# State mixing by halves, another order of its squares and subtractions, and the rotary key copies of the latents behind their squares

## What is computed

```
# layer 1: RWKV-7
xx = h_prev - h                                   # h is the normalised input, h_prev the row before
xr, xw, xk, xv, xa, xg = h + xx * mu[0..5]
r, k, v = xr @ w_r, xk @ w_k, xv @ w_v             # three 1024 x 1024 products
w_log = -softplus(-(w0 + tanh(xw @ w1) @ w2)) - 0.5   # low rank 64
a = sigmoid(a0 + (xa @ a1) @ a2)                   # low rank 64
g = sigmoid(xg @ g1) @ g2                          # low rank 128
kk = normalised per head (k * k_k);  k = k * (1 + (a - 1) * k_a)
# then the recurrence over 5 chunks of 64 frames

# layer 2: latent attention
cq, ckv, kpe = split(h @ w_in)
q = rmsnorm(cq) @ w_uq;  lat = rmsnorm(ckv);  kpe = rope(kpe)
k_nope, v = lat_all @ w_ukv;  logits = q_nope k_nope + q_pe kpe
```

## Times and profile before

| | us |
|---|---|
| timed executions | 1843.74, 1843.94, 1838.21 |
| median | 1843.74 |
| profiled execution | 1838.96 |
| its span, first to last instruction | 1837.0 |
| mean granted clock of TensorE, share of full speed | 0.961 |

### The profile page before, as it was taken

How to read it: one execution, slowest core, us unless ns; L and a number is a source line. 1 busy time by engine, 2 the same in 40 slices (tenths; PEclk the granted TensorE clock), 3 DMA queues, 4 the chain that set the end, 5 groups by cost and what they waited for, 6 DMA issues and landing times.

```text
span 1837.0 us, 37502 instructions
## 1 busy us (share of the span) xinstructions
PE 1683.1 (92%) x14117; PEld 1593.9 (87%) x14117; DVE 1169.8 (64%) x2070; ACT 856.0 (47%) x1602; POOL 731.5 (40%) x836
## 2 busy tenths in 40 slices
PE   4987999997987998999999888999999988999995
PEld 2876999995777997999999777899999876999994
DVE  3586677736467455677765538677765586677732
ACT  2344556533652343365633344465643444566532
POOL 5660466501024211266621245166621760466501
PEclk9998999998998999999999989999999998999998
DMA  6411555454230002455545211355546411555451
GB/s 158 125 48 48 159 138 159 125 150 140 71 113 29 4 10 75 118 157 140 146 142 173 71 58 47 95 158 148 141 135 172 131 48 47 156 142 156 127 145 60
DMA packets 342622, 205.04 MB, mean 112 GB/s; under 512 B 20898, under 2 KB 339640, under 8 KB 342384
## 3 DMA queue, kind: packets, MB, share of 16 engines
q1 hardware_dynamic: 338704, 196.35, 37.2%
q0 software_dynamic: 3808, 7.17, 1.4%
HBM read 200.00 MB, written 3.39 MB: 111 GB/s over the span
## 4 chain that ended last, share of the span: by engine, by line
PE 78%; DVE 10%; ACT 5%; issue 4%; POOL 3%; DMA 0%; ACTq 0%; POOLq 0%; DVEq 0%
PE bank L871 22%; PE bank L872 22%; PE bank L873 22%; PE bank L1170 4%; PE bank L882 2%; DVE lo L1940 1%; ACT hi L1468 1%; ACT LS L1502 1%; DVE LS L1985 1%; DVE LS L1994 1%; POOL vrows L627 1%; POOL lo L655 1%; PE bank L1194 1%; PE bank L938 1%; DVE xn L2174 1%
## 5 line engine op out<-in xcount | busy, mean ns | idle before, releaser
L871 PE MATMUL bank<-XH,hi 128*128 128x320 f32 (+1 forms) x1992 | 631.2, 317 | 20.8 <-DVE lo L1940 8.9
L1940 DVE TENSOR_TENSOR lo<-raw,hi 128x2048 fp32r<-128x2048 f32 (+3 forms) x201 | 425.1, 2115 | 317.1 <-ACT hi L1468 317.0
L872 PE MATMUL bank<-XL,hi 128*128 128x320 f32 (+1 forms) x1992 | 622.9, 313 | 0.0
L873 PE MATMUL bank<-XH,lo 128*128 128x320 f32 (+1 forms) x1992 | 622.0, 312 | 0.0
L871 PEld LDWEIGHTS bank<-XH,hi 128*128 128x128 f32 (+1 forms) x1992 | 378.7, 190 | 34.4 <-DVE lo L1940 17.7
L1468 ACT ACTIVATE hi<-raw 128x2048 fp32r<-128x2048 f32 (+4 forms) x205 | 359.6, 1755 | 75.3 <-PE bank L873 67.0
L872 PEld LDWEIGHTS bank<-XL,hi 128*128 128x128 f32 (+1 forms) x1992 | 379.1, 190 | 1.3
L873 PEld LDWEIGHTS bank<-XH,lo 128*128 128x128 f32 (+1 forms) x1992 | 378.7, 190 | 0.0
L691 POOL TENSOR_TENSOR upad<-upad,rstd 128x128 f32<-128x128 f32 (+1 forms) x176 | 167.2, 970 | 200.4 <-ACT upad L1548 200.4
L871 PE MATMUL bank<-GH,hi 128*128 128x322 f32 x704 | 219.2, 311 | 0.0
L872 PE MATMUL bank<-GL,hi 128*128 128x322 f32 x704 | 218.8, 311 | 0.0
(11 more groups left out here) (392 smaller groups left out, 2448.4 us busy)
## 6 DMA issues: line engine op xcount, KB each, us to landing
raw<-in_f_w_up SPq DMA_DIRECT2D x176, 512.0 KB, 4.9
raw<-in_f_w_down SPq DMA_DIRECT2D x64, 704.0 KB, 4.7
raw<-in_a_w_in SPq DMA_DIRECT2D x12, 1024.0 KB, 5.4
raw<-in_b_w_rkv SPq DMA_DIRECT2D x12, 1024.0 KB, 5.2
raw<-in_a_w_out SPq DMA_DIRECT2D x8, 1024.0 KB, 5.3
raw<-in_b_w_out SPq DMA_DIRECT2D x4, 1024.0 KB, 5.4
raw<-in_c_w_out SPq DMA_DIRECT2D x4, 1024.0 KB, 5.2
raw<-in_a_w_in SPq DMA_DIRECT2D x12, 256.0 KB, 4.3
```

Of the source, the lines that this page charges most:

```text
L871: pe.matmul(out, a, xh(k), start=(start and k == 0), stop=False)
L872: pe.matmul(out, a, xl(k), start=False, stop=False)
L873: last = pe.matmul(out, b, xh(k), start=False, stop=(stop and k == kt - 1))
L1940: dve.tensor_tensor(lo[n % 2][:, 0:w_], raw[n % 2][:, 0:w_], hi[n % 2][:, 0:w_].bitcast(F32), ALU.subtract).then_inc(w_lo, 1)
```

## The change

In state mixing:
- the six loads of the low-rank weights move from GpSimd's queue to SyncE's, behind the load of slab s0+1 and ahead of that of slab s0+2, with the same wait for the layer's input;
- VectorE normalises, subtracts and mixes four tiles and then the other four, and writes the rows of the shift state behind them; TensorE makes the low-rank products in the same two halves, ahead of the transposition of the shift rows;
- ScalarE applies the sigmoid (`middle(2)`) right behind `middle(1)` instead of behind the seven casts; the copy of the shift rows goes behind the casts;
- `key_squares(2)` and `(3)` go ahead of the split of slab s0+4, `(6)` and `(7)` ahead of four casts and the split of s0+5;
- `key_gain(0)` and `tile(12)` go between the two exponentials; GpSimd therefore waits for the second exponential at m = 0;
- `key_fans` are issued behind products 12, 13 and 14 as 2, 3 and 3 instead of 2, 2, 2, 2 behind 12 to 15; VectorE makes five `key_heads` ahead of the split of slab s0+8 instead of four, and `keys_and_rows(1)` behind the split of slab s0+9 instead of ahead of it.

In the latents GpSimd adds up the squares of `cq` before it copies the rotated keys, instead of after.

```diff
@@ SyncE @@
+            def low_rank_weights():
+                sp.wait_ge(x_done, 8 * xs_of[norm_of[1, "mix"]] + 8)
+                for dst, src in ((L1[:, :, 0:64], ...b_w1), (L1[:, :, 64:128], ...b_a1), (L1[:, :, 128:256], ...b_g1),
+                                 (L2[0:64, 0, :], ...b_w2), (L2[64:128, 0, :], ...b_a2), (L2[:, 1, :], ...b_g2)):
+                    sp.dma_start(dst, src).then_inc(lora_in, 16)
...
                     load(n)
+                    if n == first_slab[1, "mix"] + 1:
+                        low_rank_weights()
@@ GpSimd, pool_rwkv @@
-                pool.wait_ge(x_done, 8 * xs_of[norm_of[layer, "mix"]] + 8)
-                for dst, src in (...the same six...):
-                    pool.dma_start(dst, src).then_inc(lora_in, 16)
...
                     pool.wait_ge(rkv_evac, KD + m + 1)
+                    if m == 0:
+                        pool.wait_ge(decay_done, 1)
@@ GpSimd, pool_mla @@
+                squares(norm_of[layer, "cq"], 4)
+                pool.wait_ge(ssq_done, norm_base[norm_of[layer, "cq"] + 1])
                 pool.wait_ge(rope_done, Rb + 1)
                 kpe = KPE[64:96, :].rearrange("p (o n) -> p o n", o=1).to_broadcast([32, 16, T])
                 pool.tensor_copy(KC[64:96, :, PAST:KEYS], kpe).then_inc(kc_rope, 1)
                 pool.wait_ge(kc_rope, 1)
-                squares(norm_of[layer, "cq"], 4)
@@ TensorE, pe_rwkv @@
+                pe.wait_ge(lora_in, 96)
+                for z in range(2):
+                    for a in range(3):
+                        r_ = (slice(0, 64), slice(64, 128), slice(0, 128))[a]
+                        c_ = (slice(0, 64), slice(64, 128), slice(128, 256))[a]
+                        for k in range(4 * z, 4 * z + 4):
+                            pe.wait_ge(lora_mix, 12 * z + 4 * a + k % 4 + 1)
+                            last = pe.matmul(psum[4 + a][r_, 0:T], L1[:, k, c_], (LW, A, K)[a][:, k, :], start=(k == 0), stop=(k == KD - 1))
+                        if z:
+                            last.then_inc(lora_mid, 1)
                 pe.wait_ge(shift_set, 1)
                 pe.transpose(psum[3][0:16, 0:128], sho[:, :], ident).then_inc(shift_turned, 1)
-                (the same products, a outermost, all eight k of each)
...
-                fans_at = {12: (0, 1), 13: (2, 3), 14: (4, 5), 15: (6, 7)}
+                fans_at = {12: (0, 1), 13: (2, 3, 4), 14: (5, 6, 7)}
@@ ScalarE, act_rwkv @@
                 split_hi(s0 + 1)
-                act.wait_ge(shift_turned, 1)
-                act.copy(shot[:, :], psum[3][0:16, 0:128]).then_inc(shift_out, 1)
...
                 middle(1)
+                middle(2)
                 highs(0, 1, 8)
-                middle(2)
+                act.wait_ge(shift_turned, 1)
+                act.copy(shot[:, :], psum[3][0:16, 0:128]).then_inc(shift_out, 1)
...
                 tile(5)
-                split_hi(s0 + 4)
                 key_squares(2)
                 key_squares(3)
+                split_hi(s0 + 4)
                 tile(6)
...
                 tile(7)
+                key_squares(6)
+                key_squares(7)
                 highs(2, 0, 4)
                 split_hi(s0 + 5)
-                key_squares(6)
-                key_squares(7)
                 tile(8)
...
                 chain(act.activation(XX[:, :, :], HN[:, :, :], ACT.Exp, scale=-DECAY))
+                key_gain(0)
+                tile(12)
                 act.activation(HN[:, :, :], HN[:, :, :], ACT.Exp, scale=DECAY).then_inc(decay_done, 1)
-                key_gain(0)
                 key_gain(1)
-                tile(12)
                 tile(13)
@@ VectorE, dve_rwkv @@
+                def normed(z):
+                    k_ = slice(4 * z, 4 * z + 4)
+                    ...(L2161 for the four k of this half, then L2167 to L2169 on them)
+                for z in range(2):
+                    normed(z)
+                    for a, mu in enumerate((1, 4, 5)):
+                        for k in range(4 * z, 4 * z + 4):
+                            mixed((LW, A, K)[a][:, k, :], k, mu).then_inc(lora_mix, 1)
+                ...(the shift rows and onemka)
...
-                for m in range(4):
+                for m in range(5):
                     key_heads(m)
                 split_lo(s0 + 8)
-                for m in range(4, 8):
+                for m in range(5, 8):
                     key_heads(m)
...
                 keys_and_rows(0)
+                split_lo(s0 + 9)
                 keys_and_rows(1)
-                split_lo(s0 + 9)
```

More of the change, by code:

```diff
@@ L2159, in dve_rwkv @@
                 scale_of(j)
-                for k in range(KD):
-                    ins = dve.scalar_tensor_tensor(out=HN[:, k, :], in0=xT[:, k, :], scalar=gain(GAIN[j], k), in1=rstd[:, :],
-                                                   op0=ALU.mult, op1=ALU.mult)
-                chain(ins)
-                dve.tensor_copy(sho[:, 0:8], HN[:, :, 63])
-                dve.tensor_copy(sho[:, 8:16], HN[:, :, T - 1]).then_inc(shift_set, 1)
-                chain(dve.tensor_tensor(XX[:, :, 1:T], HN[:, :, 0:T - 1], HN[:, :, 1:T], ALU.subtract))
-                dve.tensor_tensor(XX[:, :, 0], V[:, VOFF["state_b_shift"]:VOFF["state_b_shift"] + 8], HN[:, :, 0], ALU.subtract)
-                chain(dve.tensor_scalar(XX[:, :, 64], HN[:, :, 64], -1.0, None, ALU.mult))
-                ka = V[:, VOFF["b_k_a"]:VOFF["b_k_a"] + 8]
-                dve.tensor_scalar(onemka[:, :], ka, -1.0, 1.0, ALU.mult, ALU.add)
+                def normed(z):
+                    k_ = slice(4 * z, 4 * z + 4)
+                    for k in range(4 * z, 4 * z + 4):
+                        ins = dve.scalar_tensor_tensor(out=HN[:, k, :], in0=xT[:, k, :], scalar=gain(GAIN[j], k), in1=rstd[:, :],
+                                                       op0=ALU.mult, op1=ALU.mult)
+                    chain(ins)
+                    chain(dve.tensor_tensor(XX[:, k_, 1:T], HN[:, k_, 0:T - 1], HN[:, k_, 1:T], ALU.subtract))
+                    dve.tensor_tensor(XX[:, k_, 0], V[:, VOFF["state_b_shift"] + 4 * z:VOFF["state_b_shift"] + 4 * z + 4], HN[:, k_, 0], ALU.subtract)
+                    chain(dve.tensor_scalar(XX[:, k_, 64], HN[:, k_, 64], -1.0, None, ALU.mult))
                 def mixed(dst, k, mu):
@@ L2175, in mixed @@
                                                     in1=HN[:, k, :], op0=ALU.mult, op1=ALU.add)
-                for a, mu in enumerate((1, 4, 5)):
-                    for k in range(KD):
-                        mixed((LW, A, K)[a][:, k, :], k, mu).then_inc(lora_mix, 1)
+                for z in range(2):
+                    normed(z)
+                    for a, mu in enumerate((1, 4, 5)):
+                        for k in range(4 * z, 4 * z + 4):
+                            mixed((LW, A, K)[a][:, k, :], k, mu).then_inc(lora_mix, 1)
+                dve.tensor_copy(sho[:, 0:8], HN[:, :, 63])
+                dve.tensor_copy(sho[:, 8:16], HN[:, :, T - 1]).then_inc(shift_set, 1)
+                ka = V[:, VOFF["b_k_a"]:VOFF["b_k_a"] + 8]
+                dve.tensor_scalar(onemka[:, :], ka, -1.0, 1.0, ALU.mult, ALU.add)
                 def mix(j, first, end):
```

8 lines of the change are left out of this document (4 added, 4 removed).

## The result

Four timed executions of each kernel, taken together on one chip: before 1843.84 us (median; 1838.21 to 1846.26), changed 1826.86 (1821.47 to 1827.17). The ratio is 0.9905, with a 95% interval of 0.9876 to 0.9934. The prediction was 1825.5, range 1818 to 1837. The profiled execution of the changed kernel took 1826.99 with a span of 1825.1 and a mean granted clock of 0.962, against 1838.96, 1837.0 and 0.961 before. So the medians are 17.0 apart and the two profiled executions 12.0.

What follows compares the result with a forecast made beforehand. TensorE, busy 92% of the span, was taken as the bound, so only its waits and lower clock could change. Gains of 7.3 + 8.6 = 15.9 from 1838.96 gave 1823.1, plus 2.4 for the median: 1825.5 us, range 1818 to 1837.

Steps and rivals of the forecast that it cites:

- the 2.4 that I had added: Total: half of the 4.8 us between the profiled execution and the median of the runs shown, taking 1823.1 to 1825.5.
- Front: State mixing up to product 0: a loss of 2.0 us, between 1.5 and 3.6, sigmoid's table load ahead of six casts.
- the 1.5 that I called certain: Front: product 0 ends at 467.4, against the end at 465.9 of the sigmoid wait that disappears; +1.5 us.
- the 0.5 that I took for the clock: Front: allowance for TensorE's clock falling while under half busy from 458 to 467; 0.5 us, ends 0 and 2.1.
- The rival of the table's drain: Front: table switch drains 1.38 us besides loading, so state mixing starts 1.4 later; 1826.9 us, chance 0.05.
- The rival of the clock: State mixing: thin work at 458 to 467 leaves TensorE at 1.2 GHz, 2.1 us per slow product; slower, chance 0.04.
- Products 6 to 11: State mixing: waits for squares go, 3.5 us gained, less a 2.1 slow product behind a 2.6 wait at product 10; 1.4.
- Products 12 to 17: State mixing: bank free earlier, product 14 at 536.8, 2.1 sooner; product 15 1.3 us sooner; VectorE free 6 us sooner.
- Products 18 and 20: State mixing: no wait at product 18, 3.8 us at product 20; gain 9.3 including earlier products' 1.4 and 1.3.
- State mixing, net 7.3: State mixing: gain of 9.3 us less the early shift of 2.0, ends 2 and 10; as the only gain, chance 0.07.
- Latents: Latents: squares no longer held by the rotary copy, 6.3 + 2.3 = 8.6 us gained; as the only gain, chance 0.11.
- The low end of 2 for products 18 and 20: State mixing: lowest gain, 2 us, from only the 1.4 and the 5.32 less the 4.1 then due elsewhere.

Runs made afterwards that it cites:

- e2: The changed kernel with the latents edit taken back, so state mixing only; median 1836.56 us, ratio 0.9971 to the kernel before.
- e10: Changed kernel with VectorE's first three operations of keys_and_rows(2) ahead of bonus(0) and the split of s0+10 right behind it; 1821.65 us, 0.9896 to before.
- e11: Changed kernel with ScalarE's two exponentials both ahead of tile(12) again and GpSimd's wait taken out; 1823.02 us, one execution.
- e7: Changed kernel with ScalarE's sigmoid and its table load behind the first eight casts, still ahead of the shifted rows' copy; 1826.19 us, 0.9910 to before.
- e5: Kernel before with only ScalarE's key_squares moved ahead of the split of s0+4 and the third set's casts; 1841.26 us, 0.999 to before.
- e6: Changed kernel with VectorE's split of s0+9 put back behind keys_and_rows(1); 1827.28 us, 0.9928 to before.
- e4: Kernel before with the tail alone: exponential behind tile(12), new fans and key_heads, s0+9 split ahead of keys_and_rows(1); 1834.80 us, 0.9955 to before.
- e9: The changed kernel itself, timed again in a later group; 1825.94 us, 0.9913 to before.
- e1: Kernel before with the latents edit alone, GpSimd's squares ahead of the rotary copy; 1830.48 us, 0.9930 to before.
- e8: Kernel before with the tail (exponentials, fans, key_heads, split of s0+9) and the latents edit, without front or squares; 1825.41 us, 0.9901 to before.
- e3: Kernel before with the front alone: weights on SyncE, norm, mixes and low-rank products by halves, sigmoid ahead of casts; 1845.71 us, 1.001 to before.

## Why the prediction was right, and where its steps were not

**The total.** From the profiled execution I worked out 1823.1, and that one took 1826.99: a gain of 12.0, not 15.9. The forecast met the median because of the 2.4 that I had added for the two pairs in which the runs shown lay: before's profiled execution was in the lower pair, the changed kernel's beside its median. The size is right, and the agreement to 1.4 us is partly luck. Of the missing 3.9, 2.1 are in state mixing; the latents gave 0.3 more than forecast, and the rest lies in unchanged code (+2.2, +0.9 and +0.9 at the end, against -2.0 in layer 3).

**Front, forecast +2.0, measured +2.1** (1.5 in e2, e10 and e11). Right in its parts: TensorE from 443.30 (442.5 to 443.6), still behind the weights; sigmoid ahead of the second cast; last `XL` at 466.85 (466.6 forecast); no wait for the sigmoid. The feared fall of the clock came, 0.76 from 464 to 474; the 1.5 that I called certain and the 0.5 that I took for the clock are what the marks at 31.44 and 32.08 show. e7 shows the mechanism that I had named. The rival of the table's drain falls: the load begins 0.02 us behind the function before it and the sigmoid 0.02 behind the load (458.67 to 458.69, 459.97 to 459.99), in e7 likewise. The 1.38 us that the Trainium skill gives in "ScalarE: Activation LUTs", section "What ACT_TABLE_LOAD costs", as draining beside the load, show in no row here. That the result is near that rival's 1826.9 is chance. The rival of the clock falls too: between the reciprocal and the recurrence the clock is at its lower level for 29.3 us, and was for 35.7 before.

**Products 6 to 11, forecast 1.4 gained, at most 2.1; measured 2.0.** The wait that I named as next came, 1.73 and not 2.6, and the clock stayed at 1.00 from 514 to 534, so the slow product that I took off there didn't come. Product 12 starts 90.2 us behind the reciprocal, as before (526.33 less 436.10; 515.41 and three times 3.57, less 435.97), so the front's 2.1 are made good. The failed step is the next one: I let that pass to product 14. There VectorE is late (the earlier trace rows shows only single rows of this chain): subtraction, reciprocal, eight scans of 5.77 together and another subtraction, 12.5 us without a gap. The chain begins when ScalarE has split s0+6, behind casts that wait for VectorE's own mixes, and it begins 1.7 later than before, with the front's loss in it. A gain of TensorE alone can't pull it: in e5 0.8 are left at product 14.

**Products 12 to 17, forecast: product 14 at 536.8 + 2.0, so 538.8; measured 540.6.** The same step, 1.8 us. I saw the two exponentials as what holds the bank; e11 shows that behind them VectorE's `key_heads` hold the fans just as long. `key_heads` were through at 548.7, and 546.7 was forecast, the difference carried on.

**Products 18 and 20, forecast the main gain: right, for half the reason.** No wait at product 18, a wait of 4.26 at product 20 (3.8 forecast). But with 2.0 for the front, product 20 was due at 568.4 and started at 571.26. And the swap, which I thought necessary, is worth about 0.8 (e6). By exclusion the fans and `key_heads` carry the tail: e6 takes out the swap, e11 the exponentials, e4 the squares and the front, each by itself, and product 18 has no wait in any of them; in e5, with the old fans, it waits 4.91 us. That is argued: a kernel with the fans and `key_heads` alone, or without them alone, was not run.

**State mixing, net 7.3 forecast, 5.2 measured** (6.1 in e2). The missing 2.1 are the 1.8 at product 14 and what follows from it.

**Latents, 8.6 forecast, 8.9 measured.** TensorE held under 1 us, the clock up, the rotary copy harmless. I had forecast a slowed subtraction of 2.94 us; beside the copy it took 5.98: 3.84 while the copy ran and 2.14, nearly its time alone, behind it. It held VectorE's next reciprocal until 1035.82, but TensorE has no wait from it; had TensorE waited for that slab, it would have been 3.7 us of the gain.

**Between the recurrence and the next part I had assumed nothing, and 2.2 were lost.** In stretches of 20 us from the recurrence on, the granted clock is 1.00 in both kernels through the first five; in the sixth it is 1.00 before and 0.95 after. The next two, before, then after:

```profile
718.10:738.10 20.00, 11.22 (x303) 10.35 (x298) 13.65 (x18) 6.78 (x8) 1.38 (x2) 0.91 0.40 120
738.10:758.10 20.00, 20.00 (x128) 20.00 (x127) 10.81 (x15) 5.50 (x6) 4.26 (x4) 0.92 0.36 106
```

```profile
713.05:733.05 20.00, 12.20 (x322) 11.25 (x318) 12.10 (x17) 6.78 (x8) 1.39 (x2) 0.84 0.39 121
733.05:753.05 20.00, 19.03 (x116) 19.06 (x117) 10.95 (x16) 5.38 (x6) 4.25 (x4) 0.86 0.33 99
```

The second column is TensorE's busy time and the third number from the end the granted clock. The stretch is sparse, 11 of 20 us, and the clock behind it differs: over all fourteen profiled executions the distance from the recurrence to the next reciprocal is between 174.8 and 177.9, from one and the same code. e10 has 174.77, and e9, the changed kernel again, 177.39; e2, with the same code up to there, has 175.27. So the 2.2 are no price of the change that any run could pin on it; why the clock returns early in one execution and late in another stays open.

**Slips of the prediction that changed nothing.** The end of the K set is 460.86 in the earlier trace rows; 460.46 is the start of product 0. The low end of 2 for products 18 and 20 doesn't follow from its own terms: 1.4 + 5.32 - 4.1 is 2.6, and 0.6 with the front's loss. And the earlier trace rows, given for the clock being back within one product behind each fall, has product 14 alone, and not what came behind it.

## What to carry to other kernels

A gain at one engine's wait is worth what the *other* engines' chains allow at the next meeting point: before adding up waits, look for the longest stretch in which the second engine has no gap (here VectorE's 12.5 us of subtractions, reciprocal and scans), and ask what starts that. A table load belongs where no engine waits for the work behind it; one of 1.28 us ahead of a row of casts cost 0.8 to 1.5 at the next common point. And where a stage's waits all end with the same engine, look into its queue for a gap followed by movable work: filling one gap of 2.43 us brought 3.4 at the recurrence (e10 against e2), more than the whole order of the squares.

## What the runs showed of the hardware

- A VectorE subtraction of 128 x 2048 took 2.29 us alone, 2.94 to 2.97 where GpSimd was at its products of 128 x 320 when it began, and 5.98 where GpSimd's broadcast copy of 32 x 5120 had begun 0.61 earlier, which itself took 4.45 with or without it. Where the subtraction began first it kept its time and GpSimd paid: a product of 0.86 took 2.99 (e6, 540.68), and a sum of 0.88 took 2.35 (changed, 1025.55). In these rows the one that began second is the one that got longer.
- TensorE's clock stayed at 1.00 through an idle time of 1.73 us with shorter ones around it (514 to 534), and fell behind one of 2.09 before. But the same wait for squares, of 2.08 to 2.10 us, was followed by a fall in before, e1 and e8 and by none in e3 and e4. The length of a wait doesn't settle it: product 20 and its sums took 5.99 us behind 3.35 us of waiting in the kernel before, and 4.46 behind 3.34 in e3.
- The attention behind the latents, unchanged, took between 143.7 us (before) and 151.9 (e3) in these executions. In e4, with 151.4, the granted clock was 0.73 and 0.61 in two stretches of 15 us (1126.4 to 1156.4) where before, at the same distance from the stage's start, has 0.89 and 1.00. A median over whole runs hides a stage's gain of that size; the stage's own marks show it.
